# Four pairs of query projections by seven half-size products, interleaved with the picking of keys

## The reference

```python
proj = h @ w_in                                   # h: 512 x 1024
q_att, c_kv, q_idx, k_idx, w_idx, ... = split(proj)
c_kv = rms_norm_2(c_kv, kv_norm_g)                # 512 x 256
rel = relu(einsum('bqhd,bsd->bqhs', q_idx, k_idx))
iscore = einsum('bqhs,bqh->bqs', rel, w_idx)      # index score, causal
_, sel = top_k(iscore, 128)                       # 128 keys of each query
s = einsum(q_lat, kv[sel]) * ATT_SCALE            # q_lat = q_att times w_uk, 8 heads of 128
o = softmax(s) @ kv[sel]
```

## Time and profile before

| | |
|---|---|
| Median of 3 runs | 2237.85 us (2234.93 to 2242.24) |
| Profiled execution | 2239.9 us, its span 2238.3 us |
| PE busy | 2159.3 us, 96% of the span |
| DVE busy | 1038.8 us, 46% |
| ACT busy | 486.4 us, 22% |
| Mean granted clock of PE | 0.988 of full speed |

### The profile page before, as it was taken

One profiled execution on the slowest core, in us unless ns is written; L12 is line 12 of the kernel. 1 busy time (PEld: TensorE's weight loads), 2 busy tenths in 40 slices (PEclk: granted clock), 3 DMA queues, 4 the chain that ended last, 5 costly groups with the idle time before them and its releaser, 6 DMA issues.

```text
span 2238.3 us, 24675 instructions
## 1 busy us (share of the span) xinstructions
PE 2159.3 (96%) x9449; PEld 1385.4 (62%) x9449; DVE 1038.8 (46%) x1924; ACT 486.4 (22%) x1045; POOL 115.0 (5%) x210
## 2 busy tenths in 40 slices
PE   8999999999999999999899989999998999999997
PEld 3447884868888444544656559888865555545552
DVE  4576665578887002295524755433545211111115
ACT  2134211122222001124435545211001100000002
POOL 0000000100100000000011100000000100000001
PEclk9999999999999999999999999999998999999999
DMA  4237131535554212211121110422352799999997
GB/s 163 75 131 254 40 111 57 180 112 179 189 185 96 90 54 93 76 57 66 48 76 57 57 57 6 160 76 95 123 234 113 297 427 429 427 424 428 427 428 292
DMA packets 45399, 385.36 MB, mean 172 GB/s; under 512 B 7065, under 2 KB 7193, under 8 KB 18649
## 3 DMA queue, kind: packets, MB, share of 16 engines
q1 hardware_dynamic: 30816, 317.39, 36.2%
q0 software_dynamic: 14176, 49.06, 6.4%
q10 hardware_dynamic: 289, 17.30, 2.2%
HBM read 369.54 MB, written 35.68 MB: 181 GB/s over the span
## 4 chain that ended last, share of the span: by engine, by line
PE 85%; DVE 5%; DMA 4%; issue 3%; ACT 2%; DVEq 1%; POOL 0%; SPq 0%; ACTq 0%; POOLq 0%
PE banks L501 28%; PE banks L614 15%; PE banks L1454 9%; PE banks L2750 8%; PE banks L2878 5%; PE banks L2763 4%; DMA arena<-in_experts 3%; PE banks L1570 3%; PE banks L1692 2%; PE banks L669 1%; PE banks L623 1%; PE banks L685 1%; DVE arena L2180 1%; PE banks L676 1%; PE banks L1501 1%
## 5 line engine op out<-in xcount | busy, mean ns | idle before, releaser
L501 PE MATMUL banks<-ring 128*128 128x256 f32 x1568 | 363.4, 379 | 3.5 <-ACT ring L577 3.0
L614 PE MATMUL banks<-arena,ring 128*128 128x512 f32 x800 | 345.7, 592 | 0.9 <-DVE arena L922 0.9
L501 PE MATMUL banks<-arena,ring 128*128 128x256 f32 x1400 | 326.4, 379 | 0.4 <-DVE banks L583 0.4
L501 PEld LDWEIGHTS banks<-ring 128*128 128x128 f32 x1568 | 297.4, 190 | 46.5 <-ACT ring L577 4.6
L1454 PE MATMUL banks<-arena,ring 128*128 128x512 f32 x656 | 290.9, 602 | 0.0
L501 PEld LDWEIGHTS banks<-arena,ring 128*128 128x128 f32 x1400 | 265.6, 190 | 38.4 <-issue 1.3
L614 PEld LDWEIGHTS banks<-arena,ring 128*128 128x128 f32 x800 | 151.9, 190 | 191.7 <-issue 189.9
L1454 PEld LDWEIGHTS banks<-arena,ring 128*128 128x128 f32 x656 | 125.0, 193 | 151.2 <-issue 150.0
L2878 PEld LDWEIGHTS banks<-arena 128*128 128x128 f32 x1024 | 119.9, 196 | 30.6 <-issue 29.4
L2878 PE MATMUL banks<-arena 128*128 128x128 f32 x1024 | 125.8, 283 | 6.1 <-issue 5.0
L1759 ACT ACTIVATE arena<-banks 128x512 f32<-128x512 f32 (+4 forms) x151 | 78.6, 532 | 228.1 <-PE banks L501 85.9
(11 more groups left out here) (378 smaller groups left out, 2178.4 us busy)
## 6 DMA issues: line engine op xcount, KB each, us to landing
ring<-in_stream SPq DMA_DIRECT2D x105, 1024.0 KB, 4.8
arena<-in_experts SPq DMA_DIRECT2D x52, 2048.0 KB, 23.4
ring<-in_experts SPq DMA_DIRECT2D x44, 2048.0 KB, 21.9
arena<-in_w_adaT POOLq DMA_DIRECT2D x48, 512.0 KB, 4.6
expert_results<-arena POOLq DMA_DIRECT2D x60, 128.0 KB, 7.3
arena<-modulation_rows POOLq DMA_DIRECT2D x5, 512.0 KB, 4.9
arena<-in_xT SPq DMA_DIRECT2D x2, 1024.0 KB, 6.0
first_result<-arena POOLq DMA_DIRECT2D x4, 512.0 KB, 2.9
```

The costliest lines, as they stand in the source:

```text
L501: m = pe.matmul(out, weights[:, k * P:(k + 1) * P], moving[:, k, :], start=first and k == 0, stop=k == 3, skip_group_check=True)
L614: m = pe.matmul(bank, c.weight(at + k), rhs(k), start=k == 0, stop=k == tiles - 1)
```

## The change

The eight `qa` jobs become four pairs. In the plan they take banks (0,1), (2,3), (4,5), (0,1), and the banks of the jobs after them rotate anew; the weight stream stays as it was, since each pair of heads filled one chunk already. On PE `pairs_pe` takes the place of eight `gemm` calls. ACT gets the four `pair_seeds`, DVE the four `weight_sums` (two of them ahead of the additions of the scores), the four `pair_upper` and the four `pair_lower`, which are placed between the rounds of picking: two rounds, then for each pair upper, a round, lower, the sums of the pair after next, a round; then the last six rounds.

```diff
+def query_pairs(c, h_sums):
+
+    return [Halves(c, ("qa", i), ("qa", i + 1), c.view(H_, DT, S), c.mixed(), h_sums) for i in range(0, HA, 2)]
@@ plan_second
-    for h in range(HA):
-        p.job("qa", h, "act", column_blocks(w, D, span(C_QA + h * P)))
+    p.rotation((6, 7), (0, 2, 4))
+    for h in range(0, HA, 2):
+        p.pair(("qa", h, "act"), ("qa", h + 1, "act"), [column_blocks(w, D, span(C_QA + n * P)) for n in (h, h + 1)])
+    p.rotation(range(BANKS))
@@ second_pe
-    for i in range(HA):
-        gemm("qa", i, lambda k: h[:, k, :], DT)
+    pairs_pe(c, pe, query_pairs(c, SECOND_SUMS))
@@ second_act
+    queries = query_pairs(c, SECOND_SUMS)
+    pair_seeds(c, a, queries[0])
     for i in range(HA):
-        put("qa", i, qa[:, i, :])
+        if i % 2 == 0 and i + 2 < HA:
+            if i:
+                put("qa", i - 1, qa[:, i - 1, :])
+            pair_seeds(c, a, queries[i // 2 + 1])
+            put("qa", i, qa[:, i, :])
+        elif i == HA - 2:
+            put("qa", i - 1, qa[:, i - 1, :])
+            put("qa", i, qa[:, i, :])
+    put("qa", HA - 1, qa[:, HA - 1, :])
@@ second_dve
+    queries = query_pairs(c, SECOND_SUMS)
+    for q in queries[0:2]:
+        weight_sums(c, v, q.n)
     wi = tokens(sm, WI_S)
...
-    for _ in range(TOPK // 8):
+
+    def take_eight():
+
         for t in range(3):
             v.max(m8[:, t, :], work[:, t, 0:(t + 2) * P])
         v.drain()
         for t in range(3):
             v.match_replace(work[:, t, 0:(t + 2) * P], m8[:, t, :], work[:, t, 0:(t + 2) * P], TAKEN)
         v.drain()
+
+    taken = 2 + 2 * len(queries)
+    take_eight()
+    take_eight()
+    for j, q in enumerate(queries):
+        pair_upper(c, v, q)
+        take_eight()
+        pair_lower(c, v, q)
+        if j + 2 < len(queries):
+            weight_sums(c, v, queries[j + 2].n)
+        take_eight()
+    for _ in range(taken, TOPK // 8):
+        take_eight()
```

## The result

| | before | changed |
|---|---|---|
| Median of 12 runs | 2237.06 us (2234.79 to 2242.43) | 2245.48 us (2242.09 to 2253.07) |
| Ratio to before | | 1.0039, 95% interval 1.0027 to 1.0052 |
| Span of the profiled execution | 2238.3 us | 2243.9 us |
| Stage: first score product to first attention step of DVE | 98.24 us | 104.85 us |
| Long stretch: first score product to the first product behind the attention | 169.03 us | 175.64 us |

The changed kernel is slower by 0.39%, 8.7 us (6.0 to 11.6). The forecast was +6.1 us, 2244.0, and the measured median lies 1.5 us above it, inside the range. It was worked out from a median before of 2237.85; the twelve runs before have 2237.06, so the step from before to changed was missed by more than those 1.5 us, by 2.3 to 2.6.

The account below looks back on a forecast made before the run. TensorE (PE), with 85% of the chain, was taken as the bound. Products -6.1, shifted scores +5.5, two stalls with restarts +5.2 and clock +1.5 made +6.1 us on 2237.85, so 2244.0; range 2239.5 to 2248.5.

Parts of the forecast that it names:

- Gain of the products: TensorE's query projections: four pairs in place of eight plain jobs give back 6.1 us, bf16 products counted.
- Sums ahead of the scores: Two weight sums on VectorE before the score additions shift Relus and score products by 5.48 us, uncovered.
- Seeds and first upper: TensorE waits in pair 0, 3.2 us at the late first upper, hiding 1.4 at the seeds; +5.2 with restarts.
- Clock: TensorE's granted clock falls behind the 3.2 us stall at the first upper, costing 1.5 us; bounds 0 and 3.4.
- Rival 1: The clock doesn't fall at the 3.2 us stall: +4.6 us, 2242.5; chance 0.27.
- rival 2: The clock stays low longer behind the stall, as at 952 to 958.7: +8.0 us, 2245.9; chance 0.10.
- VectorE's end: At the first attention score, VectorE's added work is covered by its earlier idle time, with 3.9 us left.
- Rival 3: VectorE becomes the bound at the first score, picking over 3.9 us later than worked out: about 2248; chance 0.08.
- The sum: All terms of the stage together: +6.1 us on the kernel before, median 2244.0; forecast's chance 0.45.

Follow-up runs that it names:

- retimed: Changed kernel with sums of pairs 0 and 1 moved up, first upper before any picking round, two rounds in pair 0; 0.9982 of the kernel before, -4.0 us.
- sums_alone: Kernel before, plain query projections, plus only the eight VectorE operations of two weight sums ahead of the score additions, results unused; 1.0022 of the kernel before, +4.9 us.
- early_sums: Changed kernel with the weight sums of pairs 0 and 1 moved up behind the moving sums of h; 0.9995 of the kernel before, -1.1 us.
- upper_first: Changed kernel with no picking round ahead of the first upper, the two rounds following at the end; 1.0024 of the kernel before, +5.4 us.
- filled: Changed kernel with 13 bf16 products of ones on TensorE in the stall before pair 0's third step; 1.0028 of the kernel before, +6.3 us.
- no_extra_round: The retimed kernel with one picking round, not two, behind the sums of pair 0; 0.9999 of the kernel before, -0.2 us.

## Why the prediction was right

**Gain of the products.** Held. The 176 instructions after the first upper ran with no gap but the clock, and the retimed kernel, where little else is left, gives back 4.2 us of the 6.1. Most of the other 1.9 can be read from its rows: 1.17 us of wait at the seeds and, by my estimate from rows 6, 0.25 for the restart there, 0.2 at the third step of pair 1 (16 instructions in 3.84 us where they take 3.62), and 0.2 for the score products (8.49 us against 8.33).

**Sums ahead of the scores.** Held in place and mechanism, mis-sized by 0.35: 5.83 us in place of 5.48, since VectorE paused 0.43 us in one of them. `sums_alone`, where VectorE didn't pause, and `early_sums` show the term from both sides: 5.46 in TensorE's wait (5.05 in the stage), and 5.83. One reading under it was loose: the 0.22 and 0.25 us in rows 4 are how long ScalarE had been idle, not how far a Relu came behind an addition. That VectorE released it, on which the term rests, they do show.

**Seeds and first upper.** The waits were 1.18 and 3.26 us; I had 1.45 and 3.2. That the late upper hides the seeds' wait is only worked out: removing the upper's lateness left the seeds' wait where it was (1.18 us in `upper_first`), and no run took the seeds' wait away.

**Clock.** The fall that I took by the nearest row came in all three profiles with the stall of 3.26 us (changed kernel twice, `early_sums`), and not in the filled one, nor in the three without the stall (`upper_first`, `retimed`, `no_extra_round`). It cost 1.7, I had 1.5. Rival 1 fell, and rival 2 as well: the clock was back after 3.4 us. But what I held against rival 2, that TensorE did small products at 952 and dense ones here, doesn't carry it. Behind that same wait (3.45 or 3.46 us) and the same small products the half clock lasted 6.8 us in three profiles (before, `retimed`, `no_extra_round`) and 3.4 in that of `early_sums`. Why it lasts 3.4 us at one time and 6.8 at another stays open, so that the size of the term was in part luck.

**VectorE's end.** I had 3.9 us left, the profile has 4.27, though the half clock made VectorE wait 2.62 us before lower 1 where I had 0.7. Rival 3 didn't come here, but it decides in the next step: `upper_first` and `no_extra_round` are both bound by it, and each us of it costs more than the one us that the rival counts (from `retimed` to `no_extra_round` 3.6 us in the long stretch for 2.2 in the stage).

**The sum.** +6.1 against +6.6 in the stage and +8.7 (6.0 to 11.6) and +8.1 (4.9 to 11.2) in the time. The two mis-sized terms, the sums (+0.35) and the clock (+0.2), explain the stage; the other 1.5 to 2.1 us of the time have no term. I gave the change under 0.3% the larger chance, 0.59, and slower 0.37; 0.39% lies over that line, though its interval (0.27 to 0.52) reaches under it. The forecast stood 0.6 us from the line, so these chances hung on half a us.

## What to carry to other kernels

Work that is moved into another engine's idle time is paid where that engine is the pacer, not where it is idle: two sums in the wrong one of VectorE's stretches cost nearly the whole gain of four pairs, and done 40 to 47 us earlier, where VectorE was idle, they cost nothing. When two engines hand work back and forth, put the step that the other waits for ahead of the filler, and give the filler to the places where its own engine waits; then count again which of them ends last, since one round of 3.3 us shifts the bound. The stall of TensorE has to be counted with what the clock adds: 3.26 us of waiting cost 1.7 us more behind it. And a saving is to be followed beyond the stage in which it is made: in `filled` and `upper_first` most or all of it was gone 70 us later.

## What the runs showed of the hardware

In each of the three profiles with the stall of 3.26 us a half clock of 3.4 us came behind it, with its beginning 1.2, 0.5 and 0.4 us after the restart. In the one profile with 13 bf16 products of ones in it (2.97 us) there was none. The same wait of 3.45 or 3.46 us in the scores went with a half clock of 6.8 us in three profiles and of 3.4 in a fourth:

```profile
957.00:958.00 1.00, 1.00 (x4) 0.82 (x3) 0.83 (x2) 0.90 (x2) 0.29 (x1) 0.50 0.00 0
958.00:959.00 1.00, 1.00 (x7) 0.53 (x4) 0.81 (x3) 0.76 (x3) 0.22 (x1) 1.00 0.00 0
```

These windows are from `early_sums`, where TensorE went on at 953.98; in the kernel before it went on at 952.55 and the clock was back at 958.7.

In the profile of `upper_first` the first attention, which no kernel here alters, began at half clock; in that of `retimed` it didn't. Of the other seven, the kernel before had a little of it (0.91 over the same 20 us) and the rest none (1.00). Windows of both, the first from `upper_first`:

```profile
160.00:180.00 20.00, 19.84 (x75) 14.63 (x76) 6.95 (x18) 6.06 (x16) 0.00 (x0) 0.58 1.01 319
```

```profile
160.00:180.00 20.00, 20.00 (x128) 15.07 (x127) 12.39 (x32) 9.28 (x23) 0.00 (x0) 1.00 1.00 316
```

TensorE did 75 instructions there against 128, and the next stage began 9.2 us later (237.64 against 228.46, of which 1.1 us were there before). A single profile's span can be off by more than the change that is studied: the two profiles of the changed kernel have spans of 2243.9 and 2241.2 us and a stage of 104.85 in both, and `upper_first` has a span of 2248.1 us with a shorter stage.
